# Collecting an expert group's tokens once for two rounds of a sparse expert layer

## The reference

```
g_sel = argmax(h @ w_rg + b_rg)                     # one of 4 expert groups per token
top_v, top_i = top_k(e_logits of that group, 2)     # two of its 8 experts
gate = softmax(group logits)[g_sel] * softmax(top_v)
y[token] += gate * ((silu(x @ w_gate[e]) * (x @ w_up[e])) @ w_down[e])   # for both experts e
```

## Time and profile before

| | us |
|---|---|
| median of 3 runs | 2050.36 (2040.73 to 2052.54) |
| the profiled execution | 2037.15 |
| its span, first to last instruction | 2035.4 |
| TensorE busy (page) | 1862.7, 92% |
| VectorE, ScalarE busy | 556.2, 368.1 |
| mean granted TensorE clock | 0.953 of full |

### The profile page before, as it was taken

The page is one execution under the profiler, slowest core; times in us unless marked ns, Lnnn a source line. Parts: engine busy times, 40 slices in busy tenths (PEclk is TensorE's granted clock), DMA queues, the critical chain, the costliest instruction groups (busy, mean ns, idle before and its releaser), DMA issues.

```text
span 2035.4 us, 24231 instructions
## 1 busy us (share of the span) xinstructions
PE 1862.7 (92%) x9730; PEld 949.7 (47%) x9730; DVE 556.2 (27%) x1250; ACT 368.1 (18%) x673; POOL 36.0 (2%) x60
## 2 busy tenths in 40 slices
PE   4899778699999999999999996778999999999997
PEld 2477534364444444444446773434544444444443
DVE  0154456433001110111135544554311011101112
ACT  2131134312111010101023102432210101111011
POOL 0000200000000000000000001000000000000000
PEclk9799988899999999999999988987999999999999
DMA  9722499948899999999972127995449999999994
GB/s 398 286 83 95 138 327 339 349 162 347 326 416 371 404 374 378 368 400 378 379 303 83 53 90 258 344 331 212 165 187 416 369 396 375 387 368 391 383 374 178
DMA packets 112007, 609.74 MB, mean 300 GB/s; under 512 B 13235, under 2 KB 15540, under 8 KB 50194
## 3 DMA queue, kind: packets, MB, share of 16 engines
q1 hardware_dynamic: 108690, 595.77, 74.3%
q0 software_dynamic: 3200, 12.35, 1.8%
HBM read 602.26 MB, written 5.81 MB: 299 GB/s over the span
## 4 chain that ended last, share of the span: by engine, by line
PE 78%; SPq 11%; DMA 4%; issue 3%; DVE 2%; POOLq 1%; ACT 1%; POOL 0%; DVEq 0%; ACTq 0%
PE PS L1040 33%; PE PS L603 10%; PE PS L1007 10%; PE PS L1019 7%; SPq L462 5%; SPq L457 4%; PE PS L947 4%; PE PS L531 3%; PE PS L562 2%; DMA ring<-in_w_ada 2%; DMA ring<-in_pool_kv 1%; SPq L495 1%; POOLq L389 1%; PE PS L571 1%; DMA ring<-in_w_down 1%
## 5 line engine op out<-in xcount | busy, mean ns | idle before, releaser
L1040 PE MATMUL PS<-ring,big 128*64 128x512 f32 x3072 | 680.2, 597 | 7.3 <-ACT big L1173 6.1
L1040 PEld LDWEIGHTS PS<-ring,big 128*64 128x64 f32 x3072 | 215.6, 137 | 425.9 <-issue 417.5
L1173 ACT ACTIVATE big<-PS 128x512 f32<-128x512 f32 (+8 forms) x204 | 146.9, 730 | 1089.1 <-PE PS L1040 394.8
L1503 DVE TENSOR_TENSOR big<-big,PS 128x320 f32<-128x320 f32 (+3 forms) x156 | 80.5, 522 | 687.6 <-PE PS L1019 385.1
L1007 PE MATMUL PS<-big 128*128 128x256 f32 (+1 forms) x768 | 216.0, 409 | 0.8 <-DVE big L1955 0.8
L603 PE MATMUL PS<-mT,ring 128*128 128x320 f32 x768 | 215.5, 439 | 0.0
L603 PEld LDWEIGHTS PS<-mT,ring 128*128 128x128 f32 x768 | 146.0, 192 | 62.4 <-issue 5.2
L1007 PEld LDWEIGHTS PS<-big 128*128 128x128 f32 (+1 forms) x768 | 124.6, 188 | 90.4 <-issue 82.1
L1019 PE MATMUL PS<-big 128*128 128x320 f32 x512 | 145.8, 438 | 2.2 <-ACT big L1173 2.2
L1019 PEld LDWEIGHTS PS<-big 128*128 128x128 f32 x512 | 94.8, 190 | 62.5 <-issue 22.7
L562 PE MATMUL PS<-ring,cT 128*32 128x512 f32 x384 | 56.8, 720 | 34.1 <-POOLq L389 22.7
(11 more groups left out here) (290 smaller groups left out, 1258.5 us busy)
## 6 DMA issues: line engine op xcount, KB each, us to landing
ring<-in_w_gate SPq DMA_DIRECT2D x128, 1024.0 KB, 9.5
ring<-in_w_up SPq DMA_DIRECT2D x128, 1024.0 KB, 8.9
ring<-in_w_down SPq DMA_DIRECT2D x128, 1024.0 KB, 7.8
ring<-in_pool_kv SPq DMA_DIRECT2D x256, 256.0 KB, 8.9
ring<-in_w_ada SPq DMA_DIRECT2D x48, 1024.0 KB, 13.3
big<-in_windows SPq DMA_DIRECT2D x16, 2432.0 KB, 8.4
ring<-in_w_in SPq DMA_DIRECT2D x24, 1024.0 KB, 7.2
ring<-in_w_out SPq DMA_DIRECT2D x8, 1024.0 KB, 10.2
```

The costliest lines, as they stand in the source:

```text
L1040: i = mm(PS[SLOTS * x:SLOTS * x + SLOTS, out_bank + half, :], stationary(k, x), w, start=(k == 0), stop=(k == steps - 1))
L1173: return nc.scalar.activation(out, in_, ACT.Copy)
L1503: return V.tensor_tensor(out, a, b, op)
```

## The change

A round pair shares one expert group, E = 4 l + g // 2. A new 0/1 tile `member` (tokens by up to 128 members) is made once per expert group; TensorE's new `members` collects with it that group's tokens into `rows` (128 members by 1024 channels) and their slot ranks and gates into `of_member`, for the first group in `stage_out` and for each further one in the odd round before it. `gather` then needs one product per chunk, from rows. pick, wpick and spread have 128 members instead of 320 tokens. `slot_sums` sums slots into members (two products per half of the channels), VectorE keeps the sum of both rounds in `sums`, and the new `back` takes it to the 320 tokens, once per pair: in the next even round behind `up(0)`, and behind the last round for the last pair. Slot sums stand behind `gate(0)` as one block. `crowded` is set too where an expert group has more than 128 tokens. The buffers in `big` are laid out anew, and three unused semaphores go.

```diff
 SLOTS, GE = 64, 4
+MEMBERS = 128
...
+            member = L3(8960, 3, MEMBERS)
+            pick = big[:, 9344:9600]
+            wpick = big[:, 9600:9856]
+            spread = L3(9856, 2, MEMBERS)
+            of_member = big[:, 10112:10176]
             hsel = L3(10496, 8, GE * SLOTS)
+            rows = big[:, 12544:13568]
+            outs = L3(13568, 2, 1024)
+            sums = mT_[:, 0:1024]
+            back = rt[:, 0:T]
...
@@ tensor engine: stage_out @@
-                    mod_turn(23)
-                    keep_warm(4)
-                    pe.wait_ge(sem["mods_kept"], 1)
-                else:
-                    keep_warm(2)
-                pe.wait_ge(sem["gates_kept"], l + 1)
+                    mod_turn(23)
+                keep_warm(2)
+                members(HALF * l, PS[:, 0, 0:64], 5)
+                pe.wait_ge(sem["gates_kept"], l + 1)
+                if l == 0:
+                    pe.wait_ge(sem["mods_kept"], 1)
                 for part in ((0, 1), (2, 3), (4, 5, 6, 7)):
                     gather(GROUPS * l, part)
+            def members(E, where, bank):
+                pe.wait_ge(m["members"], E + 1)
+                for t, (t0, n) in enumerate(SPANS):
+                    i = mm(where, moe.member[0:n, t, :], moe.place[0:n, t, 4:68], start=(t == 0), stop=(t == 2))
+                i.then_inc(m["members_mm"], 1)
+                for h in range(2):
+                    for t, (t0, n) in enumerate(SPANS):
+                        i = mm(PS[:, bank + h, :], moe.member[0:n, t, :], moe.htok[0:n, t, h * 512:(h + 1) * 512], start=(t == 0), stop=(t == 2))
+                    i.then_inc(m["members_mm"], 1)
             def gather(G, chunks):
+                pe.wait_ge(m["members_kept"], 3 * (G // 2) + (3 if chunks[-1] >= 4 else 2))
                 pe.wait_ge(m["picks"], G + 1)
                 for k in chunks:
-                    for t, (t0, n) in enumerate(SPANS):
-                        i = mm(PS[:, k // 2, (k % 2) * 256:(k % 2) * 256 + 256], moe.htok[0:n, t, k * 128:(k + 1) * 128],
-                               moe.pick[0:n, t, :], start=(t == 0), stop=(t == 2))
+                    i = mm(PS[:, k // 2, (k % 2) * 256:(k % 2) * 256 + 256], moe.rows[:, k * 128:(k + 1) * 128], moe.pick, start=True, stop=True)
                 i.then_inc(m["gather_mm"], 1)
+            def slot_sums(G):
                 pe.wait_ge(m["slot_out_copied"], 2 * G + 2)
+                for h in range(2):
+                    for pair in range(2):
+                        i = mm(PS[:, 6 + h, :], moe.spread[:, pair, :], moe.outs[:, pair, h * 512:(h + 1) * 512], start=(pair == 0), stop=(pair == 1))
+                    i.then_inc(m["slot_sum_mm"], 1)
+            def back(E):
+                pe.wait_ge(m["sums_kept"], 4 * E + 4)
+                for d in range(8):
+                    if d >= 2:
+                        pe.wait_ge(m["back_added"], 8 * E + d - 1)
+                    mm(PS[:, 6 + d % 2, 0:T], moe.sums[:, d * 128:(d + 1) * 128], moe.back, start=True, stop=True).then_inc(m["back_mm"], 1)
...
@@ tensor engine: group @@
                 gate(0)
                 if prev:
-                    slot_sums(G - 1, range(0, 4))
+                    slot_sums(G - 1)
                 up(0)
-                if prev:
-                    slot_sums(G - 1, range(4, 8))
-                pe.wait_ge(m["weighted_picks"], G + 1)
-                for pair in range(2):
+                if g % 2 == 0:
+                    if prev:
+                        back(E - 1)
+                    pe.wait_ge(m["weighted_picks"], G + 1)
+                    for pair in range(2):
+                        tr(PS[:, 4, pair * 128:(pair + 1) * 128], M.wpick[:, pair * 128:(pair + 1) * 128])
                     for t, (t0, n) in enumerate(SPANS):
-                        i = tr(PS[:, 4 + pair, t0:t0 + n], M.wpick[0:n, t, pair * 128:(pair + 1) * 128])
-                i.then_inc(m["spread_turned"], 1)
+                        i = tr(PS[:, 5, t0:t0 + n], M.member[0:n, t, :])
+                    i.then_inc(m["spread_turned"], 1)
+                else:
+                    pe.wait_ge(m["sums_kept"], 2 * G)
+                    pe.wait_ge(m["weighted_picks"], G + 1)
+                    for pair in range(2):
+                        i = tr(PS[:, 7, pair * 128:(pair + 1) * 128], M.wpick[:, pair * 128:(pair + 1) * 128])
+                    i.then_inc(m["spread_turned"], 1)
+                    if more:
+                        pe.wait_ge(m["spread_copied"], G + 1)
+                        members(E + 1, PS[:, 7, 256:320], 4)
                 gate(1)
...
-                    slot_sums(GROUPS * l + GROUPS - 1, range(8))
+                    slot_sums(GROUPS * l + GROUPS - 1)
+                    back(HALF * l + HALF - 1)
...
@@ scalar engine @@
+            def keep_members(E, where, bank):
+                act.wait_ge(m["members_mm"], 3 * E + 1)
+                copy(moe.of_member, where).then_inc(m["members_kept"], 1)
+                for h in range(2):
+                    act.wait_ge(m["members_mm"], 3 * E + 2 + h)
+                    copy(moe.rows[:, h * 512:(h + 1) * 512], PS[:, bank + h, :]).then_inc(m["members_kept"], 1)
...
@@ vector engine @@
+                c(ts(Mo.km[:, 1:2], Mo.km[:, 1:2], float(MEMBERS), None, ALU.is_gt))
+                c(tt(Mo.km[:, 0:1], Mo.km[:, 0:1], Mo.km[:, 1:2], ALU.max))
                 V.tensor_copy(crowded[:, :], Mo.km[:, 0:1]).then_inc(sem["crowd_known"], 1)
                 dve.wait_ge(sem["gates_turned"], l + 1)
                 V.tensor_copy(Mo.gT[0:32, :], PS[0:32, 1, 0:T]).then_inc(sem["gates_kept"], 1)
+                picks(l, 0)
...
+            def members(l, e):
+                E = HALF * l + e
+                if e:
+                    dve.wait_ge(m["spread_turned"], 2 * E - 1)
+                tt(moe.member, spread(K("iota"), 1, 3), spread(moe.ranks[:, :, e], 2, MEMBERS), ALU.is_equal).then_inc(m["members"], 1)
...
+            def slot_sums(l, g):
+                G = GROUPS * l + g
+                for h in range(2):
+                    part = moe.sums[:, h * 512:(h + 1) * 512]
+                    dve.wait_ge(m["slot_sum_mm"], 2 * G + h + 1)
+                    if g % 2:
+                        tt(part, part, PS[:, 6 + h, :], A_).then_inc(m["sums_kept"], 1)
+                    else:
+                        V.tensor_copy(part, PS[:, 6 + h, :]).then_inc(m["sums_kept"], 1)
+            def back(E):
                 for d in range(8):
+                    dve.wait_ge(m["back_mm"], 8 * E + d + 1)
+                    tt(moe.y[:, d, :], moe.y[:, d, :], PS[:, 6 + d % 2, 0:T], A_).then_inc(m["back_added"], 1)
```

More of the change, by code:

```diff
@@ L1088, in group @@
                     gather(G + 1, (2, 3))
+                if g % 2 and more:
+                    pe.wait_ge(m["members_kept"], 3 * E + 6)
                 pe.wait_ge(m["spread_copied"], G + 1)
@@ L1292, in keep_page_tokens, with out @@
                 keep_tokens(l, 4, vC, 4)
-            def out(b, bank, c0, name):
+            def out(b, bank, c0):
                 for hh in range(2):
                     src = PS[64 * hh:64 * hh + 64, bank, 256:352].rearrange("p (c n) -> p c n", c=2)[:, :, 8 * hh:8 * hh + 8]
-                    i = copy(mT[64 * hh:64 * hh + 64, c0:c0 + 2, SEQ + b * 8:SEQ + b * 8 + 8], src)
-                i.then_inc(sem[name], 1)
+                    copy(mT[64 * hh:64 * hh + 64, c0:c0 + 2, SEQ + b * 8:SEQ + b * 8 + 8], src)
             def seq_logits(l, b):
@@ L1315, in pages_out @@
                 act.wait_ge(sem["c_out_mm"], 8 * l + b + 1)
-                out(b, 7, 4, "c_out_copied")
+                out(b, 7, 4)
             def unit_logits(l, b):
@@ L1427, in group @@
                 act.wait_ge(m["spread_turned"], G + 1)
-                copy(M.spread, PS[:, 4:6, 0:T]).then_inc(m["spread_copied"], 1)
+                if g % 2 == 0:
+                    copy(M.back, PS[:, 5, 0:T])
+                copy(M.spread.rearrange("p a n -> p (a n)"), PS[:, 7 if g % 2 else 4, 0:256]).then_inc(m["spread_copied"], 1)
+                if g % 2 and g < GROUPS - 1:
+                    keep_members(HALF * l + g // 2 + 1, PS[:, 7, 256:320], 4)
                 act.wait_ge(used, pairs + 12)
@@ L1982, in group, with hidden @@
                     dve.wait_ge(m["spread_turned"], G)
-                for j, (t0, n) in enumerate(SPANS):
-                    gate = Mo.gt[0:n, j, g * GE:g * GE + GE]
-                    i = tt(Mo.wpick[0:n, j, :].rearrange("p (e s) -> p e s", e=GE), Mo.pick[0:n, j, :].rearrange("p (e s) -> p e s", e=GE),
-                           spread(gate, 2, SLOTS), M_)
-                    if j < 2:
-                        c(i)
-                i.then_inc(m["weighted_picks"], 1)
-                if g < GROUPS - 1:
-                    dve.wait_ge(m["weighted_picks"], G + 1)
+                tt(by_slot(Mo.wpick), by_slot(Mo.pick), spread(Mo.of_member[:, 32 + g * GE:32 + g * GE + GE], 2, SLOTS),
```

(24 more changed lines are left out.)

96 lines of the change are left out of this document (43 added, 53 removed).

## The result

The changed kernel takes **1959.11 us**, the median of four runs (1951.85 to 1965.66), the kernel before in the same comparison 2047.14 (2040.73 to 2052.54). The ratio is 0.957, its 95% interval 0.9522 to 0.9619. The prediction was 1958 in 1930 to 1996. The profiled execution took 1965.66 us, with a span of 1963.9; it is the slowest of the four. Of all runs told of here one execution is left out, 3587.47 us of the kernel with its slot sums done twice, whose other three lie within 3.4 us of each other.

What follows compares the result with a forecast made beforehand. TensorE bounds the kernel before, weight loads the changed one. Stretches falling to 469 us give 84.9, plus 8.0 ahead, minus 6.6 behind: 86 off, 1951 from the profiled time or 1964 from the median; 1958 taken between, range 1930 to 1996.

Steps and rivals of the forecast that it cites:

- loads' term: Expert stretch of a layer, first gate product to last down product: weight loads at 421.5 GB/s need 469 us.
- TensorE's 447: Same stretch: TensorE's own work after the change needs 447 us a layer, at 58.2 us a group.
- Gather 4.4: Gather in each group: eight products instead of 24, 4.4 us, 8.9 less per group.
- Members 6.3: Collecting a pair's tokens: three narrow products and six of 512 columns per two groups, 6.3 us.
- Ahead of the layer: Before the first gate product: members 6.3 plus gather 4.4 replace 13.46 us; about 4 us earlier per layer, 8 in all.
- Behind the layer: From the last slot sums to the end: 13.1 us instead of 9.8, 3.3 more per layer, 6.6 in all.
- The sum: Whole kernel: 84.9 from the stretches plus 8.0 ahead minus 6.6 behind, 86 us off.
- (a): Expert stretch: TensorE stays the bound because loads run faster than any wide row; 447 us a layer, 1907; chance 0.04.
- (b): Load queue not kept full, dips stay in part; at 400 GB/s 493 us a layer, whole 2000 to 2013; chance 0.14.
- (c): Expert stretch can get only today's 380 GB/s; 511 to 519 us a layer, no gain, 2036 to 2063; chance 0.04.
- (d): TensorE's clock falls in the new waits, slower than before; with ten cold passes a group 2180; chance 0.04.
- (e): An expert group of over 128 tokens sends its layer down the dense path; about 3200; chance 0.02.

Runs made afterwards that it cites:

- the repeated kernel: The changed kernel run once more unaltered, as the base for the last versions beside it: 1958.83 us, ratio 0.960 to the kernel before.
- one part alone: Against the kernel before: slots summed over the 128 collected tokens, but still gathered from all 320 tokens by 24 products: 2041.68 us, ratio 1.000.

## Why the prediction was right, and where its terms were off

**The bound.** Right. The loads' term of 469 us a layer measured 472.4 and 471.9, TensorE's 447 measured 446.4 and 446.6 (stretch to the last down product's end, less the weight waits), the pair of groups 119 measured 119.24. The waits that the prediction put at 22 us a layer were 26.0 and 25.2. The rate of 421.5, taken from the two wide rows, came out as 421. The experiments with fewer bytes and with fewer products show that it is a floor, some 3 us higher than the sum. Three rows of layer 0, the ninth load's issue, a window from it and the last half pass, show where the 3 us lie:

```profile
551.39 4.24 SPq L489 DMA_DIRECT2D ring<-in_w_gate  x4
```

```profile
551.39:1012.37 460.98, 433.22 (x1862) 162.82 (x1860) 43.19 (x80) 55.22 (x75) 0.00 (x0) 1.00 1.01 419
```

```profile
1014.81 3.65 PE L1061 MATMUL PS<-ring,big 128*64 128x512 f32 x16 [1.02 <-DMA ring<-in_w_down]
```

The issue is 5.4 us behind the first gate product, as predicted. At 419 GB/s the window holds the 192.9 MB; it is 461.0 us where the prediction had 1.7 + 457.7 = 459.4. The last half pass then begins 2.4 us later; the prediction had put 1.0 there for the landing, with no row behind it.

**The products.** Gather 4.4: measured 0.96 + 0.96 + 1.82 = 3.74: twice four instructions (the first from 634.90 to the next pass at 635.86) and eight from 651.45 to 653.27. An instruction takes 0.23 to 0.24 where the row of before had a mean of 0.277; that mean was over tiles of 128 and 64 tokens, and the new gather has none of 64. Members 6.3: measured 627.39 - 620.51 = 6.88, at 0.494 for a wide instruction instead of the 0.454 of the keep-warm products; the products of members do have a tile of 64. Back 5.7: measured 684.58 - 679.24 = 5.34. Copy wait 0.8: measured 0.47. Slot sums 3.6: 3.63. Together TensorE's own part of the pair is 119.24 less 3.8 of load waits, 115.4 for the predicted 116.5; none of this decides once the loads are late. The layer's 447 is met more closely than its terms: four pairs at 115.4, less 20.1 for what the ends lack as measured, plus 1.7 are 443, about what the kernel with less to load takes.

**Ahead of the layer.** In layer 1 the prediction's 4 us came (14.77 from the end of the router's products to the first gate product instead of 18.8). In layer 0 only 0.35 came (18.7 from the keep-warm products on instead of 19.03). Of the prediction's terms this one fell furthest short in the profiled execution:

```profile
527.33 3.76 PE L550 MATMUL PS<-xT 128*128 128x512 f32 x4
530.88 1.57 PE L1013 MATMUL PS<-big 128*128 128x64 f32 x6
532.38 7.94 PE L1017 MATMUL PS<-big 128*128 128x512 f32 x12
540.25 3.72 PE L1025 MATMUL PS<-big 128*128 128x256 f32 x16
546.01 15.65 PE L1061 MATMUL PS<-ring,big 128*64 128x512 f32 x64 [2.03 <-ACT big L1206]
```

Four keep-warm instructions take 3.76 us, twice the full-clock pace, and members' first ones are slow too; the pair above has 6.00 for the twelve that take 7.94 here. The granted clock is 0.50, the level of 1.2 GHz, from 527.33 to 534.00; ahead of that TensorE had stood for 2.68 us up to 520.32, and it was 0.50 from there on too. In the profiled execution of the repeated kernel it is 1.00 there, the first four of these rows take 1.96, 0.92, 6.00 and 3.72, and it is 16.3 us from the first of them to the gate pass; in six traces of the experiments with the same start it is 15.9 to 16.7, at 1.00 too. So the half clock belongs to the one execution, and the change brings some 2.7 us there instead of 4. What is lacking is a longer stand ahead of the gate pass: 3.99 us in the repeated kernel and 3.6 to 4.4 in those six, where before had 2.05. ScalarE's copy of the gathered slots ends 2.1 us before that pass in the repeated kernel; what the rest waits for the traces don't show.

**Behind the layer.** Predicted 3.3 us more in each, measured 1.9 in layer 0: from the last slot sums' start to VectorE's last operation 1031.27 - 1019.57 = 11.7 against 9.8. The second of the eight chunks on VectorE in the changed kernel, and the start of the third:

```profile
1025.69 0.48 DVE L1553 SCALAR_TENSOR_TENSOR xT<-PS,modT,xT 128x256 f32<-128x256 f32 x1
1026.08 0.21 DVE L1547 TENSOR_TENSOR rr<-PS,modT 128x64 f32<-128x64 f32 x1
1026.33 0.23 DVE L1547 TENSOR_TENSOR xT<-xT,rr 128x64 f32<-128x64 f32 x1
1026.48 0.48 DVE L1553 SCALAR_TENSOR_TENSOR xT<-PS,modT,xT 128x256 f32<-128x256 f32 x1
```

A chunk takes 1026.48 - 1025.69 = 0.79 us and not 0.95: with back's products ahead of it VectorE's operations run one behind the other, and overlap where the sum of their durations had been taken.

**The sum.** Between the two profiled executions the stretches give -78.6 (38.2 and 40.4), the tails +3.8, the starts -4.4: -79, where the prediction had -86. The spans differ by 71.5. The other 7.7 us lie outside the experts, where little was changed (layer 0's keep-warm products start 8.6 us later); executions of the one kernel lie 13.8 us apart. By medians the gain is 88, so the choice of 1958 between 1951 and 1964 met 1959 by the half-way mark and not by a term.

**The rivals.** (a), TensorE stays the bound at 1907: it is what the kernel with less to load does, 1900.91, and not what this one does. (b), the queue not kept full, hardly happened here: between the ninth load and the last the windows of 10 us bring 418 to 427 GB/s, but for the three behind members at 405, 387 and 397. It did in the runs with more work on TensorE, at 484 to 491 us a layer, so its mechanism is real, and the prediction's argument against it (with TensorE ahead of its loads, free halves wait for loads) holds only while TensorE's need lies well under the loads': 25 us under was enough, 0 to 5 us were not. (c), 380 GB/s as the ceiling, fell: 414 and 410 over whole stretches. By the Trainium skill, "HBM Reference", Specifications (TRN2), 358 GB/s is a core's share when both cores of a pair stream, and one that streams alone gets about 425; the trace of this kernel, on one core, agrees with the second figure at 421. (d), the clock: 1.00 in both stretches, in spite of 48 waits of at most 1.8 us. (e), the dense path, did not occur.

## What to carry to other kernels

Before taking work off a busy engine, compute what the next resource needs for the same round. Here TensorE was cut by 64 us a layer and the gain was 39, since the loads at 421 GB/s were only some 39 below it. Two needs that come close don't give the larger of the two: with TensorE at 467 to 473 us and the loads at 472, the layer took 484 to 491, as the ring ran empty in one part of a round and full in another. The distance alone doesn't settle it, since with TensorE 43 to 46 us above the loads, by slot sums done four times in one block, 14 us of load waits stayed, while the kernel before, some 40 above, had 1.3 us in all; so look at where in a round the work without weights stands. And when a change has two parts, ask what each leaves as the work that stands ahead of a wait; one part alone, as it was built here, was worth nothing for such a reason.

## What the runs showed that was not expected

- **The size of a load.** A full queue of loads of 1024 KB brings 421 GB/s, of 512 KB of the same weights 409. In the latter the runs that are contiguous in a partition are 4096 bytes instead of 8192, by the kernel's slices.
- **The half clock after a short wait.** After 2.77 us of standing, 48 gather instructions stayed at 0.50 granted clock for 25 us, TensorE busy throughout, while the first gate pass loses 1.7 us after a wait of 2.03. Why the one lasts so long and the other does not, these runs don't show.
- **A tile of 64 partitions.** Products summed over three tiles, one of them of 64 tokens, cost more for each instruction than those over full tiles: 0.277 against 0.23 us for 256 columns, 0.494 against 0.454 for 512. No run was made for this, but the starts of single instructions show where it lies. In the 256-column rows of before at 583.15 they are 0.216 us apart within the full tiles, and 0.31 to 0.32 at four starts in six: the two of the tile of 64 and the two behind it. In members' 512-column rows it is 0.429, and 0.52 to 0.53 at the same four.
